# One expert pair with 96 and 32 slots, experts visited in an order made on the chip, and a reordered retention stage

## The reference, cut to what matters

```python
# mixture of experts: 256 tokens, 32 experts, each token takes its best 4
logits = (xt @ w_router + b_router)
top_val, top_idx = lax.top_k(logits, 4);  gates = softmax(top_val)
counts = segment_sum(ones, top_idx)               # tokens of each expert
hcat = xb @ w_in[e] + b_in[e]                     # w_in[e]: 1024 x 2048
act = x_glu * sigmoid(1.702 * x_glu) * (x_lin + 1)
y = act @ w_out[e] + b_out[e]                     # w_out[e]: 1024 x 1024
# retention, 4 heads of q, k width 256 and v width 512
o = (decayed q k^T) v
oc = o - mean(o);  o = oc * rsqrt(mean(oc * oc) + EPS)
return (silu(g) * o) @ w_out                      # w_out: 2048 x 1024
```

## Time and profile before

| | |
|---|---|
| median of three runs | 2144.73 us (2140.66 to 2172.89) |
| the profiled execution's own time | 2144.41 us |
| its span in the trace | 2142.6 us |
| PE busy | 1998.6 us, 93% of the span |
| DVE, ACT, POOL busy | 628.5, 406.0, 177.7 us |
| expert pairs on PE | from 276 to 1209 us; the job to 1241 us |
| retention steps | from 1421 to 1477 us |

### The profile page before, as it was taken

How to read it: one execution, slowest core, us unless ns; L and a number is a source line. 1 busy time by engine, 2 the same in 40 slices (tenths; PEclk the granted TensorE clock), 3 DMA queues, 4 the chain that set the end, 5 groups by cost and what they waited for, 6 DMA issues and landing times.

```text
span 2142.6 us, 24188 instructions
## 1 busy us (share of the span) xinstructions
PE 1998.6 (93%) x9788; PEld 1273.0 (59%) x9788; DVE 628.5 (29%) x1299; ACT 406.0 (19%) x764; POOL 177.7 (8%) x231
## 2 busy tenths in 40 slices
PE   6999999888998999888988999999999999989998
PEld 4644654433334444333333566688788888868887
DVE  2867422211122221222113255431104216310321
ACT  3125211110111111111110121230113224320210
POOL 0000000000000000000000000000654931000000
PEclk9999999999999999999999999999999999989999
DMA  9986789999999999999999985833343342634220
GB/s 364 349 306 227 278 367 397 422 425 425 428 426 426 426 428 426 418 427 424 424 427 426 410 324 207 341 118 138 119 151 124 138 157 94 221 118 157 108 108 20
DMA packets 122568, 627.83 MB, mean 293 GB/s; under 512 B 5281, under 2 KB 9505, under 8 KB 94337
## 3 DMA queue, kind: packets, MB, share of 16 engines
q1 hardware_dynamic: 121168, 619.10, 72.5%
q0 software_dynamic: 1328, 7.73, 1.0%
HBM read 625.76 MB, written 1.05 MB: 293 GB/s over the span
## 4 chain that ended last, share of the span: by engine, by line
PE 73%; DMA 14%; DVE 7%; issue 3%; ACT 2%; SPq 1%; DVEq 0%; ACTq 0%
PE psum L1023 32%; PE psum L1361 23%; DMA ring<-in_w_in_dram 13%; PE psum L1034 3%; PE psum L1339 2%; PE psum L1493 1%; PE psum L1250 1%; PE psum L1123 1%; DVE arena L2428 1%; PE psum L1668 1%; PE psum L1062 1%; DMA ring<-in_w_ada_dram 1%; DVE arena L2443 1%; PE psum L1642 1%; PE psum L1328 1%
## 5 line engine op out<-in xcount | busy, mean ns | idle before, releaser
L1361 PE MATMUL psum<-ring,arena 128*64 128x512 f32 x3120 | 710.6, 606 | 70.7 <-DMA ring<-in_w_in_dram 70.0
L1023 PE MATMUL psum<-arena,ring 128*128 128x256 f32 (+1 forms) x3072 | 683.9, 385 | 6.1 <-ACT arena L1747 6.1
L1023 PEld LDWEIGHTS psum<-arena,ring 128*128 128x128 f32 x3072 | 585.0, 191 | 103.1 <-issue 23.9
L1361 PEld LDWEIGHTS psum<-ring,arena 128*64 128x64 f32 x3120 | 245.3, 140 | 518.3 <-issue 518.3
L1880 ACT ACTIVATE arena<-psum 128x512 f32<-128x512 f32 (+1 forms) x155 | 88.5, 571 | 811.4 <-PE psum L1361 702.0
L2428 DVE TENSOR_TENSOR arena<-psum,arena 128x512 f32<-128x512 f32 (+1 forms) x68 | 42.8, 669 | 409.0 <-PE psum L1382 399.2
L2415 DVE TENSOR_SCALAR arena<-consts,arena 128x64 f32<-128x64 f32 (+1 forms) x68 | 16.7, 310 | 333.3 <-PE psum L1361 333.3
L2702 DVE SCALAR_TENSOR_TENSOR consts<-psum,smalls,consts 128x255 f32<-128x255 f32 (+1 forms) x88 | 38.4, 478 | 232.2 <-ACT consts L2025 231.4
L1339 PE MATMUL psum<-arena 128*128 128x256 f32 (+1 forms) x288 | 70.4, 387 | 12.1 <-DVE arena L2404 10.7
L2882 POOL DMA_DIRECT2D arena<-in_pos_dram x1 | 0.5, 543 | 934.6 <-PE psum L1472 934.6
L1787 ACT ACTIVATE arena<-psum 128x512 f32<-128x512 f32 (+1 forms) x53 | 29.6, 561 | 232.5 <-PE psum L1023 175.2
(11 more groups left out here) (382 smaller groups left out, 1609.2 us busy)
## 6 DMA issues: line engine op xcount, KB each, us to landing
ring<-in_w_in_dram SPq DMA_DIRECT2D x129, 2048.0 KB, 14.9
ring<-in_w_out_dram SPq DMA_DIRECT2D x66, 2048.0 KB, 17.1
ring<-in_w_ada_dram SPq DMA_DIRECT2D x36, 2048.0 KB, 12.9
ring<-in_w_up_dram SPq DMA_DIRECT2D x22, 2048.0 KB, 7.9
ring<-in_w_ret_dram SPq DMA_DIRECT2D x12, 2048.0 KB, 15.1
ring<-in_w_down_dram SPq DMA_DIRECT2D x16, 1408.0 KB, 5.9
ring<-in_w_qkv_dram SPq DMA_DIRECT2D x4, 2048.0 KB, 20.3
ring<-in_w_rout_dram SPq DMA_DIRECT2D x4, 2048.0 KB, 10.0
```

The source lines that it names most:

```text
L1023: ins = nc.tensor.matmul(bank(c)[:, at:at + n], w[:, k, m * P:m * P + P], r, start=(k == 0), stop=(k == k_tiles - 1))
L1361: ins = nc.tensor.matmul(psum[at:at + CAP, p, :], act[:, k, CAP * e:CAP * e + CAP], w, start=(k < 3 - halves), stop=(k >= KD - 3 + halves))
```

## The change

There are two changes in one.

**Experts.** Pairs 0 and 1 are still experts 0 to 3. For the other 28 experts, `order_experts` on VectorE ranks them by count, and writes an order: the fullest first, the emptiest second, then the rest by falling count. Pair 2 (`WIDE_PAIR`) gives the fullest 96 slots and the emptiest 32. To that end the fullest expert's `slot_of` is lowered by 32 and its count too, the emptiest's raised by 32, and `slots` begins at -32. On PE the wide pair's `rows` uses four matmuls of 32 columns where the others use two of 64. SP and DVE load the expert numbers of each pair from SBUF into registers. Jobs are still made for counts above 64 (96 for the fullest), after the counts are changed.

**Retention.** Scores are made two heads ahead into two buffers. ACT no longer copies the output: DVE multiplies it from PSUM straight into the gate (`ro`). GpSimd adds the squares of the four tiles (512, then 256 columns), and PE sums one tile in `rvar` instead of four. `rvar` of head h-1 comes after `ro` of head h, and `rout` waits for one head for every four tiles.

```diff
+WIDE_PAIR = 2
+WIDE = 96
+NARROW = P - WIDE
+LEAD = WIDE - CAP
+SORTED = E - 2 * WIDE_PAIR
@@ def retention_steps():
-    steps = [("rs", 0), ("sums", 7)]
+    steps = [("rs", 0), ("sums", 7), ("rs", 1)]
     for h in range(RET_HEADS):
         steps += [("ro", h, 0), ("ro", h, 1)]
-        if h < RET_HEADS - 1:
-            steps += [("rs", h + 1), ("rvar", h)]
+        if h:
+            steps += [("rvar", h - 1)]
+        if h + 2 < RET_HEADS:
+            steps += [("rs", h + 2)]
     return steps + [("cols", 7), ("rout", 0), ("rvar", RET_HEADS - 1), ("rout", 1)]
@@ SP
+            sp.wait_ge(order_ready, 1)
             with sp.Fori(2, PAIRS) as i:
+                of_pair = [sp.value_load(order[0:1, bass.ds(i * 2 + h, 1)], min_val=0, max_val=E - 1) for h in range(2)]
                 for j in range(12):
                     pair_left(i, j)
-                    load(MOE_0 + j, expert_source(i * 2 + j % 2, j // 2))
+                    load(MOE_0 + j, expert_source(of_pair[j % 2], j // 2))
@@ PE
+                tiles = [(CAP * e, CAP, e) for e in range(halves)]
+                if wide:
+                    tiles = [(NARROW * q, NARROW, int(NARROW * q >= WIDE)) for q in range(P // NARROW)]
...
-                        for e in range(halves):
-                            at = CAP * (e if halves == 2 else k % 2)
+                        for n, size, e in tiles:
+                            at = n if halves == 2 else CAP * (k % 2)
                             w = tile(halves * j + e, k_tiles, kk, BANK * (p - banks[0]))
-                            ins = nc.tensor.matmul(psum[at:at + CAP, p, :], act[:, k, CAP * e:CAP * e + CAP],
+                            ins = nc.tensor.matmul(psum[at:at + size, p, :], act[:, k, n:n + size],
                                                    w, start=(k < 3 - halves), stop=(k >= KD - 3 + halves))
...
                 if kind == "rout":
-                    pe.wait_ge(ret_done, RET_HEADS - 1)
                     arrived(step)
-                    rout_tiles(h, 0, 12)
+                    for k in (0, 4, 8):
+                        pe.wait_ge(ret_done, k // 4 + 1)
+                        rout_tiles(h, k, k + 4)
...
-                    pe.wait_ge(ret_sq, h + 1)
-                    for k in range(4):
-                        ins = nc.tensor.matmul(half(step, 0), con("ones"), sq[:, k, :],
-                                               start=(k == 0), stop=(k == 3))
+                    pe.wait_ge(ret_sq_summed, h + 1)
+                    ins = nc.tensor.matmul(half(step, 0), con("ones"), ret_sums[:, 0, :], start=True, stop=True)
@@ ACT
                     if c == 0 and h:
-                        read_ready(act, ("rvar", h - 1))
-                    if c == 0 and h >= 2:
-                        act.wait_ge(ret_done, h - 1)
+                        act.wait_ge(ret_sq_paired, h)
                     read_ready(act, step)
-                    ins = nc.scalar.activation(flat(sq[:, 2 * c:2 * c + 2, :]), bank(step), ACT.Square)
-                    if c == 1:
-                        ins.then_inc(ret_sq, 1)
-                    copy(step, ro_of[h % 2][:, 2 * c:2 * c + 2, :])
+                    nc.scalar.activation(flat(sq[:, 2 * c:2 * c + 2, :]), bank(step), ACT.Square).then_inc(ret_sq, 1)
@@ DVE
+            def order_experts():
+                dims = [P, SORTED, SORTED]
+                count_of, ids = count[:, 2 * WIDE_PAIR:E], con("experts")[:, 2 * WIDE_PAIR:E]
+                own.link(V.scalar_tensor_tensor(out=key_of, in0=count_of, scalar=float(E), in1=ids,
+                                                op0=ALU.mult, op1=ALU.add))
+                own.link(V.tensor_tensor(pairwise, over_tiles(key_of, SORTED), key_of.unsqueeze(2).to_broadcast(dims),
+                                         ALU.is_gt))
+                own.link(V.tensor_reduce(rank_of, pairwise, AX_X, ALU.add))
...
+                own.mark(V.scalar_tensor_tensor(out=count_of, in0=is_cold, scalar=float(CAP - NARROW), in1=count_of,
+                                                op0=ALU.mult, op1=ALU.add))
+                own.mark(V.scalar_tensor_tensor(out=slot_of[:, :, 2 * WIDE_PAIR:E], in0=over_tiles(is_cold, TT),
+                                                scalar=float(CAP - NARROW), in1=slot_of[:, :, 2 * WIDE_PAIR:E],
+                                                op0=ALU.mult, op1=ALU.add))
...
+                V.tensor_copy(order[:, 2 * WIDE_PAIR:E], order_f).then_inc(order_ready, 1)
...
+                    if wide:
+                        for h, (at, size, _) in enumerate(shares(2, b, wide)):
+                            bb = bias[:, h, 4 * c:4 * c + 4].unsqueeze(2).to_broadcast([P, 4, size])
+                            ins = V.tensor_tensor(dst[:, :, at:at + size], src[:, :, at:at + size], bb, ALU.add)
...
+            order_experts()
             experts(moe, 2, 0, (0, 1), 0, (2, 3), 0, first=True)
-            with dve.Fori(1, PAIRS - 1) as i:
-                experts(moe, 2, i, (i * 2, i * 2 + 1), 0, (i * 2 + 2, i * 2 + 3), 0)
+            hot_and_cold = pair_at(WIDE_PAIR)
+            experts(moe, 2, 1, (2, 3), 0, hot_and_cold, 0, next_wide=True)
+            experts(moe, 2, WIDE_PAIR, hot_and_cold, 0, pair_at(WIDE_PAIR + 1), 0, wide=True)
+            with dve.Fori(WIDE_PAIR + 1, PAIRS - 1) as i:
+                experts(moe, 2, i, pair_at(i), 0, pair_at(i + 1), 0)
...
+                elif kind == "ro":
+                    c = step[2]
+                    dve.wait_ge(ret_sq, 2 * h + c + 1)
...
+                    g = flat(rg[:, 4 * h + 2 * c:4 * h + 2 * c + 2, :])
+                    read_done(V.scalar_tensor_tensor(out=g, in0=bank(key), scalar=0.5, in1=g, op0=ALU.mult,
+                                                     op1=ALU.mult), key)
                 elif kind == "rvar":
...
-                    own.link(V.tensor_tensor(o, o, over_tiles(y, 4), ALU.mult))
                     g = rg[:, 4 * h:4 * h + 4, :]
-                    V.scalar_tensor_tensor(out=flat(g), in0=flat(o), scalar=0.5, in1=flat(g), op0=ALU.mult,
-                                           op1=ALU.mult).then_inc(ret_done, 1)
+                    V.tensor_tensor(g, g, over_tiles(y, 4), ALU.mult).then_inc(ret_done, 1)
@@ POOL
+            pool.wait_ge(ret_qk, 8)
+            for h in range(RET_HEADS):
+                pool.wait_ge(ret_sq, 2 * h + 2)
+                if h:
+                    read_ready(pool, ("rvar", h - 1))
+                G.tensor_tensor(ret_sums, sq[:, 0:2, :], sq[:, 2:4, :], ALU.add).then_inc(ret_sq_paired, 1)
+                pool.wait_ge(ret_sq_paired, h + 1)
+                G.tensor_tensor(ret_sums[:, 0, :], ret_sums[:, 0, :], ret_sums[:, 1, :], ALU.add
+                                ).then_inc(ret_sq_summed, 1)
```

More of the change, by code:

```diff
@@ L490, in transformer_blocks_kernel @@
         gates_t = cut(T)
+        order = cut(E).bitcast(I32)
         assert cut.at <= ARENA - KD * E
+        pairwise = flat(tanh_e)[:, 0:SORTED * SORTED].rearrange("p (a b) -> p a b", b=SORTED)
+        key_of, rank_of, is_hot = (cum[:, SORTED * n:SORTED * n + SORTED] for n in range(3))
+        is_cold, place_of, order_f = (flat(flags)[:, SORTED * n:SORTED * n + SORTED] for n in range(3))
         sums_of = b_out_sb.rearrange("p (k n) -> p k n", n=P)
@@ L1341, in scatter, with experts @@
                     ins.then_inc(s.x_ready, 1)
-            def experts(s, halves, i, full, tile, first=False):
+            def experts(s, halves, i, full, tile, first=False, wide=False):
                 width = CAP * halves
+                tiles = [(CAP * e, CAP, e) for e in range(halves)]
+                if wide:
+                    tiles = [(NARROW * q, NARROW, int(NARROW * q >= WIDE)) for q in range(P // NARROW)]
                 def rows(j, act, k_tiles, n_slabs, banks, j0):
@@ L2396, in add_scattered, with pair_at @@
+            def pair_at(i):
+                return tuple(dve.value_load(order[0:1, bass.ds(i * 2 + h, 1)], min_val=0, max_val=E - 1)
+                             for h in range(2))
             def add_scattered(s, base, first):
@@ L2405, in add_scattered, with experts @@
                     ins.then_inc(s.x_free[c % 2], 1)
-            def experts(s, halves, i, experts_of, b, next_experts, next_b, first=False):
+            def experts(s, halves, i, experts_of, b, next_experts, next_b, first=False, wide=False, next_wide=False):
                 width = CAP * halves
```

81 lines of the change are left out of this document (54 added, 27 removed).

## The result

The changed kernel takes 2109.43 us (median of 4 runs, 2104.59 to 2111.0), the kernel before beside it 2143.18 (median of 4, 2140.66 to 2172.89). The ratio is 0.983 with a 95% interval of 0.981 to 0.986: a gain of 1.7% that is sure, and just under the 2% that count as faster. The profiled execution took 2109.2 us with a span of 2107.4.

A forecast was written before the change was run, and what follows sets the result against it. Transfers bound the expert pairs, PE's own chain what follows. From 2144.4 us, 32.1 for the job and 5.8 for the retention come off, with the rest hidden: 2106.5 us, range 2099 to 2115.

The forecast's parts named there:

- What bounds the kernel: Pairs 2 to 15 go at the transfers' pace, PE having some 5 us slack each; after the job PE's chain bounds.
- The job goes: After pair 15: no count above 64 remains, so no job runs and the last scatter starts 32.1 us sooner.
- the sign that the prediction named: End of the experts: PE's scatter of the last pair was to come about 0.8 us behind `down(5)`.
- the price of the branches: Engines branching past the job's code: a possible stall priced at 0 to 2 us.
- Slabs behind the last scatter: First projection's slab was to arrive by 1215 us, wanted at 1222.4: hidden with 7 us left.
- ACT's load of the count: Between ACT's last copy and the norm's squares: 0.46 us that fits in, taken as nothing, at worst 1 us.
- `order_experts`: DVE passes starting at 269.2 us: about 7 us, hidden in 14.0 us of idle time with 7 left.
- The wide pair: Pair 2: 384 instructions at 0.114 us; with bias additions 3.2 us more, inside the 5 us slack, so nothing.
- The rivals of narrow matmuls one or two at a time: Wide pair's matmuls do not overlap four deep: two at a time 2144 us (0.01), one at a time 2226 (0.01).
- Retention: First score to projection: stall gone and four variances 1.3 us shorter, less 0.5 of waits; 5.8 us gain, 3.5 to 6.7.
- POOL's share of 6.9 us: Retention: POOL active 6.9 of some 22 us, so DVE's chain may lengthen by up to 0.8 us a head.
- More than the sum: Rival, pairs over some 820 us: a transfer rate 0.7% above 424 GB/s gives 6 us, 2100 us; chance 0.09.

The follow-up runs named there:

- the masks first: Changed kernel with PE's job branch moved ahead of up(3) of pair 15, and each head's DVE mask put before the preceding variance: 2107.6 us, ratio 0.985.
- the two kernels with the job dropped: Kernel before, job threshold raised by 32 so no job runs: 2113.53 us; the same with 223 more instructions starting PE's program: 2125.28 us, one run.
- the kernel with the experts only: Changed kernel with the retention of the kernel before: 2110.2 us, ratio 0.986.

## Why the prediction was right

The forecast was 2106.5 us in a range of 2099 to 2115; the median is 2109.43.

- **What bounds the kernel** held: the pairs at the transfers' pace (67.1 us of waits for 70.0), PE behind them.
- **The job goes**: the right mechanism with a term mis-sized. The copy behind `down(5)` and the 0.77 us to the scatter came as worked out in three kernels with the job's code shortened, left out or moved (18.9 us for the stretch, 32.0 less than before, predicted 32.1). In the changed kernel the branch cost 3.7 us, and the sign that the prediction named, a scatter about 0.8 us behind `down(5)`, failed: it came 3.1 behind. The step that failed is the price of the branches: I took nothing for PE's, from rows of branches back at the end of pairs, which land on code that was just run; the skip lands on code that was not. The Trainium skill, "Runtime: NRT & Kernel Launch", section Instruction fetch mechanics, says that a taken branch whose target is not in the prefetched window waits until the target is fetched; the branch of 6.2 us with a fetch inside it agrees in kind. My bound of 0 to 2 us came from the gap between ACT and PE, which says nothing on what a branch takes (6.2 us here, of which 2.4 show), and it left out the clock, 1.3 of the 3.7.
- **Slabs behind the last scatter**: no wait for one, as laid out.
- **ACT's load of the count**: nothing, as taken.
- **`order_experts`**: 6.6 us for 7, and 7.3 of idle time left for 7. Its passes of 784 columns took 0.97 us, as estimated.
- **The wide pair**: 0.110 us an instruction for 0.114, hidden. The rivals of narrow matmuls one or two at a time are out, in all 16 pairs too.
- **Retention**: 6.0 us for 5.8, with two errors that nearly cancel. PE's own work before the projection is 20.1 us for 20.3, and the wait for head 3's mask 0.95 for 0.5. (The prediction lets the projection start at 20.5; its own terms give 20.3 + 0.5 = 20.8, and its gain of 6.2 uses them rightly. It started at 21.05. POOL's share of 6.9 us there is 6.7 by its own terms; no other number hangs on either.) That mask stands behind head 0's refinement, which POOL's additions lengthened by 0.65 us; I had given DVE up to 0.8 a head and counted it covered by the slack of the last head, which this wait does not have. The Trainium skill, "SBUF — State Buffer", section Who interferes with whom, says that a VectorE instruction with two SBUF inputs contends with a GpSimd one that reads SBUF; the trace agrees, with 0.42 us against 0.66 and 0.83.
- **More than the sum** did not come, but the spread behind it is real: the experts' stretch took 2.6 us less in this pair of traces, and 915.1 to 924.8 us in all.

The 3.7 us of the branch were too few to leave the range, and in the profiled executions they went under by luck: the two stretches ahead happened to be 3.2 us shorter, the last one 2.2 longer.

## What to carry to other kernels

Code that is skipped at run time is not free. A forward branch took PE 0.35 or 6.2 us here, by where it landed; what shows of it is what PE's queued work and the waits behind it do not cover (0 or 2.4 us), and up to 2.2 more for the clock. Look for a small loss with no releaser in the profile among the sequencer's records of that line, and test it by moving the code. To take work off the engine that is the bound, look where the bound changes hands: the job was worth its 32 us because it lay behind the last slab of the pairs, and inside them it would have been worth nothing. Before a step is put earlier in a queue, count what then comes later: the masks first took one wait away and made two.

## What the runs showed of the hardware

- A forward branch past 110 instructions of the program (380, with a matmul as four) took PE's sequencer 6.2 to 6.3 us in four kernels and 0.35 in four others, by the place of the code. PE stood idle for 3.1 to 3.2 us in the first and for no more than the usual 0.8 in the second. One fetch of instructions (16 KB: 0.88 MB in 54 on the page of the kernel after) starts within each branch of 5.9 us or more.
- The branches back in the loop over pairs, over 574 instructions by the same count, stayed short: 0.08 to 0.24 us in the kernel after, and no fetch on that queue between 482 and 1206 us, while PE went round that loop.
- The low clock does not follow each such stand: after 3.13, 3.17 and 3.16 us idle the scatter took 5.69, 5.40 and 6.57 us, after 3.09 us 4.36. And stops of 1.49 and 1.50 us in the retention were enough in the two kernels with the job dropped (12.31 us for 48 instructions), while 1.50 us in the earlier trace rows and in the kernel with the experts only was not (10.63).
- Four tiles of 32 columns run as fast as two of 64 also where they multiply the same slab: 128 instructions in 13.94 us, 64 in 13.95.
- DVE operations of 256 columns with both inputs in SBUF went from 0.42 to 0.66 us beside a POOL addition of 512 columns and to 0.83 beside one of 256, and POOL's of 512 from 1.27 to 1.65 us beside a DVE pass of 1024.
